# The first four modulation blocks of a two-block transformer: half of each block's rows multiplied by TensorE from the landing buffer

## What is computed

```python
c_silu = jax.nn.silu(c)
for layer in range(DEPTH):
    mods = jnp.split(c_silu @ ada_w[layer] + ada_b[layer], N_MOD, axis=-1)
    sh, sc, g = mods[0], mods[1], mods[2]
    h = modulate(rms_norm(x, norm_g[layer, 0]), sh, sc)
    x = x + MACARON_WEIGHT * (1.0 + g)[:, None, :] * swiglu(h, ffn_w_in[layer, 0], ffn_w_out[layer, 0])
    ...
```

## Time and profile before

| | us |
|---|---|
| median of three executions | 1636.21 |
| lowest and highest | 1634.9 and 1637.21 |
| span of the profiled execution | 1632.3 |
| TensorE busy in it | 1408.4 (86%) |
| VectorE busy in it | 1282.2 (79%) |
| ScalarE, GpSimd busy in it | 628.4 (38%), 352.7 (22%) |

### The profile page before, as it was taken

How to read it: one execution, slowest core, us unless ns; L and a number is a source line. 1 busy time by engine, 2 the same in 40 slices (tenths; PEclk the granted TensorE clock), 3 DMA queues, 4 the chain that set the end, 5 groups by cost and what they waited for, 6 DMA issues and landing times.

```text
span 1632.3 us, 27592 instructions
## 1 busy us (share of the span) xinstructions
PE 1408.4 (86%) x10538; PEld 1319.3 (81%) x10538; DVE 1282.2 (79%) x1730; ACT 628.4 (38%) x933; POOL 352.7 (22%) x332
## 2 busy tenths in 40 slices
PE   3899994899998899999857999998879767875897
PEld 2799994899997699999737999998858646754796
DVE  6998778887776887877665777755777899999674
ACT  3333334343335343333534433345435411332343
POOL 7992002000000100000000000000550388776000
PEclk9999997999999999999879999999979877987899
DMA  9688772587763658775305687753412222122452
GB/s 361 244 286 308 293 273 100 214 307 303 294 220 103 236 214 330 276 276 201 102 13 193 218 297 272 230 181 123 160 35 82 74 78 76 54 78 61 128 186 65
DMA packets 65212, 308.03 MB, mean 189 GB/s; under 512 B 7248, under 2 KB 8560, under 8 KB 58864
## 3 DMA queue, kind: packets, MB, share of 16 engines
q1 hardware_dynamic: 65136, 307.00, 53.6%
HBM read 305.92 MB, written 1.05 MB: 188 GB/s over the span
## 4 chain that ended last, share of the span: by engine, by line
PE 67%; DVE 27%; issue 3%; ACT 2%; DMA 1%; DVEq 0%; POOL 0%; SPq 0%; ACTq 0%; POOLq 0%
PE tiles L325 16%; PE tiles L326 15%; PE tiles L327 15%; PE acc L325 5%; PE acc L326 5%; PE acc L327 5%; DVE w_lo L317 5%; DVE arena L1428 4%; PE mods L413 2%; DVE arena L1049 2%; PE acc L529 1%; DVE arena L1424 1%; DVE arena L1423 1%; DVE rh L1234 1%; DMA arena<-in_gstream 1%
## 5 line engine op out<-in xcount | busy, mean ns | idle before, releaser
L317 DVE TENSOR_TENSOR w_lo<-land,w_hi 128x1024 fp32r<-128x1024 f32 x391 | 491.4, 1264 | 201.1 <-ACT w_hi L313 200.9
L325 PE MATMUL tiles<-x_hi,w_hi 128*128 128x256 f32 x1976 | 584.9, 296 | 66.1 <-DVE x_lo L1107 33.0
L313 ACT CAST w_hi<-land 128x1024 fp32r<-128x1024 f32 x391 | 408.3, 1045 | 586.8 <-PE tiles L327 418.7
L326 PE MATMUL tiles<-x_lo,w_hi 128*128 128x256 f32 x1976 | 568.0, 287 | 0.0
L327 PE MATMUL tiles<-x_hi,w_lo 128*128 128x256 f32 x1976 | 567.5, 287 | 0.0
L325 PEld LDWEIGHTS tiles<-x_hi,w_hi 128*128 128x128 f32 x1976 | 386.4, 196 | 83.3 <-issue 66.1
L326 PEld LDWEIGHTS tiles<-x_lo,w_hi 128*128 128x128 f32 x1976 | 388.4, 197 | 2.0 <-issue 1.9
L327 PEld LDWEIGHTS tiles<-x_hi,w_lo 128*128 128x128 f32 x1976 | 387.9, 196 | 0.0
L1049 DVE SCALAR_TENSOR_TENSOR arena<-arena,csil 128x512 f32<-128x512 f32 x280 | 215.2, 768 | 2.0
L325 PE MATMUL acc<-h_hi,w_hi 128*128 128x256 f32 x704 | 200.2, 284 | 4.1 <-DVE h_lo L1068 4.1
L326 PE MATMUL acc<-h_lo,w_hi 128*128 128x256 f32 x704 | 199.7, 284 | 0.0
(11 more groups left out here) (245 smaller groups left out, 1774.9 us busy)
## 6 DMA issues: line engine op xcount, KB each, us to landing
land<-in_stream SPq DMA_DIRECT2D x391, 512.0 KB, 4.1
arena<-in_gstream SPq DMA_DIRECT2D x46, 2048.0 KB, 8.6
x<-in_x_t SPq DMA_DIRECT2D x1, 1024.0 KB, 14.2
arena<-in_ssm_c SPq DMA_DIRECT2D x1, 1024.0 KB, 6.7
arena<-in_ssm_b SPq DMA_DIRECT2D x1, 1024.0 KB, 4.7
out_t<-x SPq DMA_DIRECT2D x8, 128.0 KB, 1.9
cons<-in_cons SPq DMA_DIRECT2D x1, 656.5 KB, 9.1
cons<-in_mask SPq DMA_DIRECT2D x1, 256.0 KB, 4.6
```

The costliest lines, as they stand in the source:

```text
L313: nc.scalar.copy(w_hi[:, u % RING], land[:, u % LAND]).then_inc(hi_done, 1)
L317: nc.vector.tensor_tensor(w_lo[:, u % RING], land[:, u % LAND], w_hi[:, u % RING].bitcast(F32), ALU.subtract).then_inc(lo_done, 1)
L325: nc.tensor.matmul(outs, lh, rh, start=first, stop=False, **kw)
L326: nc.tensor.matmul(outs, lh, rl, start=False, stop=False, **kw)
```

## The change

For the first four blocks the products of row groups 4 to 7 (`G_HALF` = 4) move to TensorE. A new function `first_block` takes the place of `reduce_block` there. It waits until the block has landed, and issues 16 matmuls whose stationary operand is a 128x128 piece of `g_land` itself and whose moving operand is the column of `csil`; then it waits for VectorE's sum of groups 0 to 3, and adds its partition sums with the four matmuls of before, into the same columns of PSUM. VectorE does four instructions for such a block instead of eight. Since TensorE reads the landing buffer too, and last, the loads of blocks 2 to 5 now wait for `g_red` of the block two before, and no longer for `g_done`.

```diff
+G_HALF = 4
...
-                if b >= 2:
+                if b >= G_PRE + 2:
                     sp.wait_ge(g_done, i * 2 + (b - 1))
+                elif b >= 2:
+                    sp.wait_ge(g_red, b - 1)
                 sp.dma_start(g_land[:, b % 2], gstream[i * 2 + b]).then_inc(g_landed[b % 2], 16)
...
+            def first_block(b):
+
+                pe.wait_ge(g_landed[b % 2], 16 * (b // 2 + 1))
+                for q in range(4):
+                    for k in range(8 - G_HALF, 8):
+                        nc.tensor.matmul(mods[:, 4 * b + q:4 * b + q + 1], g_land[:, b % 2, k, q * P:(q + 1) * P],
+                                         csil[:, k:k + 1], start=(q == 0 and k == 8 - G_HALF), stop=False,
+                                         skip_group_check=True)
+                pe.wait_ge(g_done, b + 1)
+                for q in range(4):
+                    m = nc.tensor.matmul(mods[:, 4 * b + q:4 * b + q + 1], g_acc[:, b % 2, q * P:(q + 1) * P],
+                                         ones[:, 0:1], start=False, stop=True, skip_group_check=True)
+                m.then_inc(g_red, 1)
+
...
+            pe.wait_ge(csilu_done, 1)
             pe.wait_ge(one_in, 16)
-            reduce_block(0)
-            reduce_block(1)
+            first_block(0)
+            first_block(1)
             sum_squares(0)
             for b in range(2, G_PRE):
-                reduce_block(b)
+                first_block(b)
             ffn(0, 0)
...
+                last = 7 - G_HALF if b < G_PRE else 7
...
-                                           op1=ALU.add).then_inc(g_done if k == 7 else g_step, 1)
+                                           op1=ALU.add).then_inc(g_done if k == last else g_step, 1)
 
             def g_block(b):
-                for k in range(8):
+                for k in range(8 - G_HALF if b < G_PRE else 8):
                     g_part(b, k, "silu")
```

More of the change, by code:

```diff
@@ L1047, in g_part @@
                 else:
-                    dve.wait_ge(g_step, i * 14 + (7 * b + k))
+                    steps = (7 - G_HALF) * b if b < G_PRE else 7 * b - G_HALF * G_PRE
+                    dve.wait_ge(g_step, i * 14 + (steps + k))
                     V.scalar_tensor_tensor(out=acc, in0=rows, scalar=cv, in1=acc, op0=ALU.mult,
-                                           op1=ALU.add).then_inc(g_done if k == 7 else g_step, 1)
+                                           op1=ALU.add).then_inc(g_done if k == last else g_step, 1)
             def g_block(b):
-                for k in range(8):
+                for k in range(8 - G_HALF if b < G_PRE else 8):
                     g_part(b, k, "silu")
```

## The result

The changed kernel takes 1642.31 us in the median of eight executions (1639.8 to 1644.31); the kernel before, beside it, 1636.77 (1634.9 to 1640.79, eight executions). The ratio is 1.0033 with a 95% interval of 1.0021 to 1.0045: slower by 0.33%, 5.5 us. The span of the profiled execution went from 1632.3 to 1638.3 us.

A forecast was written before the change was run, and what follows sets the result against it. The prediction took the chain of modulation blocks to bound the start, up to 37 us, with TensorE becoming its pace. Block 3's later sum, +8.6, less GpSimd's 1.0, gave +7.6 on 1636.2: 1643.8 us, range 1633.3 to 1646.5.

The forecast's parts named there:

- rival 2: First four blocks: clock low in blocks 0 and 1, high in 2 and 3; +4.2 us, 1640.4 us; chance 0.23.
- TensorE becomes the engine that works off the blocks: First four blocks: 40 records take TensorE 8.7 us at low clock, 4.7 at high, against VectorE's 2.9.
- The clock is low in blocks 0 and 1: Blocks 0 and 1: TensorE runs at 1.2 GHz, 0.213 us a record, from 9.5 to 27.0 us.
- Rival 1: Clock rises in block 0, so no loss: around 1634.1 us, within 0.2%; chance 0.32.
- the inference from the earlier trace: Opening blocks: matmuls that use little of the array would not raise TensorE's clock; inferred from a fall behind thin work.
- The loads slip and the squares behind them: Block 2's load goes out at 18.3 us, block 3's at 27.0; the sum of squares runs 27.0 to 32.7.
- The clock falls again 5.2 us behind the squares: Early in block 3, at 37.9 us: 36 records at the low rate, its sum ending at 45.5, +8.6 us.
- What is hidden: Opening: the norm's root, the later weight units and block 4's load would add no time to the path.
- What GpSimd gives back, 1 us: Opening: GpSimd gets ahead and slows VectorE less on the path; 1 us taken, bounds nothing to 2 us.
- TensorE busy without a gap behind 75 us: After the opening: nothing else on TensorE moves there except by the shift.
- Rival 4, dearer records: New matmuls cost more than those on `mods`, sharing a buffer with VectorE; some 10% for another 2 us; no chance given.

The follow-up runs named there:

- heat: Changed kernel plus 22 matmuls of 512 columns on a constant on TensorE ahead of block 0; median 1639.69 us, ratio 1.0019 to the kernel before.
- half6: Changed kernel with six row groups of each of the first four blocks on TensorE instead of four; 1655.48 us in one execution.
- before_red: Kernel before with only the wait changed: loads of blocks 2 to 5 wait for g_red instead of g_done; ratio 1.0005.
- last1_late: Kernel before with only block 3 in the new form, four row groups on TensorE, and GpSimd's tables begun later; 1629.74 us, ratio 0.9951.
- half2_late: Changed kernel with two row groups of each of the first four blocks on TensorE, and GpSimd's tables begun later; 1628.1 us, ratio 0.9936.
- after_late: Changed kernel with GpSimd's tables begun only after four tiles of the first feed-forward; 1635.89 us, ratio 1.0000 to the kernel before.
- hold: Changed kernel plus 22 matmuls of 512 columns ahead of block 0 and eight more inside each of the four blocks; ratio 1.0051.

## Why the prediction was right

The forecast was 1643.8 us, +7.6; measured are 1642.31, +5.5, with an interval from +3.4 to +7.4. So the direction and the mechanism are as forecast and the size is somewhat too large: +7.6 lies just outside the interval, and rival 2's +4.2 is as near to the +5.5. It is the trace that decides between the two, and not the time.

- **TensorE becomes the engine that works off the blocks**: yes. 40 records take 8.5 us at the low clock (8.7 forecast) and 4.5 at the high one (4.7).
- **The clock is low in blocks 0 and 1**: yes. 17 us of one-column matmuls did not raise it, and `heat` shows that it is the clock which doubles their price. Rival 1 is out. The Trainium skill, page "TensorE: Matmul & The Clock Gate", section "What you observe", has the rise about 4 us into sustained matmul activity; here a stretch of one-column matmuls four times that long had none. The section's example is of back-to-back matmuls of another shape and type, so it gives a shape after all, and the run goes against the sentence only if that is read as holding for any matmul. For these matmuls the measurement decides for the inference from the earlier trace rows.
- **The loads slip and the squares behind them**: forecast 18.3, 27.0 and 27.0 to 32.7; measured 18.1, 26.6 and 26.5 to 31.9. The squares took 5.4 us instead of 5.7.
- **The clock falls again 5.2 us behind the squares**: it fell 4.8 us behind, at 36.7. Block 3 took 8.1 us, as forecast. (The forecast's sum has 0.15 us for the last record where 0.35 belongs; that is 0.2 us.) Rival 2 is out in the profiled execution. The coefficient step came at 44.29, +7.2 against +8.6; the missing 1.4 us is 0.5 each from the squares' start and their length, 0.3 from block 2 and 0.1 from the step in the kernel before.
- **The moment of the fall was in part luck**: 5.2 us is no fixed delay. Worked out from the windows in the same way, it was 4.8 to 5.8 us in eight of the fourteen profiled kernels, and 2.1 to 2.9 us in the other six (`heat`, `half6`, `before_red`, `last1_late`, `half2_late`, `after_late`). Both occur whether TensorE was mostly idle behind the squares (5.2 us in the kernel before, 2.7 in `before_red`) or had thin matmuls only (4.8 in the changed kernel, 2.9 in `after_late`). The rise moves too: in `after_late` 11 records fall into the 4.3 us from 26.7 to 31.0, so the clock was still low for most of them, where it had risen 3.9 us behind the first of the squares in the kernel before. These two moments make 3.2 of the 3.4 us by which the coefficient step comes later there than in the changed kernel, with the same work of TensorE up to it.
- **What is hidden**: the root, the weight units (ScalarE had the first at 37.3 us) and block 4's load were.
- **What GpSimd gives back, 1 us**: this term is the part of the forecast whose mechanism was wrong, and that it came out small was luck. I held that its large operations would still meet the feed-forward. They met the norm steps, cost 4.4 us there and 2 us more through TensorE's low clock, and were missing later, which gave 6.7 us back. Up to the second norm the balance is 0.4 us given back, within the bounds of 0 and 2. With late tables both the 4.4 and the 2 us are gone: from the coefficient step to the first h_lo the two kernels then take 14.3 us each, where with early tables it is 15.5 and 21.7. The rest of the difference to the span (+6.9 there, +6.0 at the end) is spread over 1400 us and not traced to anything. The prediction has TensorE busy without a gap behind 75 us; in the kernel before that is so up to 200 us. From 200 to 260 it is busy for 55.8 of 60 us, and from 260 to 400 for 117.3 of 140, so the time can move there by more than the shift.
- **The median against the profile**: the medians differ by 5.5 us with early tables and 8.8 with late ones, the coefficient steps by 7.2 and 10.6. The executions of the changed kernel scatter by 4.5 us, those of the kernel before by 5.9. That the clock's rise and fall, at other moments in each execution, make the scatter is a guess and was not shown.
- **Rival 4, dearer records**: no, they cost what those on `mods` do.

## What to carry to other kernels

A gap on TensorE is room only at the rate at which it will run there: cost a moved product from a row of the same shape in the same clock state, and ask what raises that clock and what lets it fall. Here thin matmuls, one column behind each 128x128 weight load, ran at 1.2 GHz for all the 17 us of blocks 0 and 1, and where the clock was high, it fell within 5 us of them. And before moving work off an engine, look whether a third one makes it slow: here a later start for tables that nobody needed yet was worth 9 us, where moving half of the products cost 5.5.

## What I had not expected

- The clock fell within 5 us from 2.4 to 1.2 GHz under one-column matmuls, with TensorE busy until it fell (`heat`), and even with eight matmuls of 512 columns among the 40 thin records of a block (`hold`: 0.50 for 18.6 us at 100% busy).
- GpSimd's operations of 128x512 stretch VectorE's 128x256 steps from 0.47 to between 1.27 and 1.49 us, some three times. And TensorE stayed at 1.2 GHz for 8.7 us, from 55.3 to 64, in which matmuls of 256 columns kept it busy for 8.4.
- Over the opening, that overlap costs 8 us wherever it falls: 222.9 and 222.6 us from the coefficient step to the second norm with early tables, 214.8 and 214.7 with late ones.
